# Expert weight units of four row blocks by 512 columns, and the fourth remainder of a group split between two engines

## The reference, cut to what matters

```python
order = jnp.argsort(flat_e)
tok = order // TOP_K
sizes = jnp.bincount(flat_e, length=N_EXPERTS).astype(jnp.int32)
xs = t[tok]
hid = jax.nn.silu(lax.ragged_dot(xs, w1, sizes)) * lax.ragged_dot(xs, w3, sizes)
y = lax.ragged_dot(hid, w2, sizes) * top_p.reshape(-1)[order][:, None].astype(h.dtype)
```

## Time and profile before

| what | value |
|---|---|
| median of 3 timed runs | 6221.68 us (6217.64 to 6225.43) |
| the profiled execution, its own time | 6225.65 us |
| its span, first to last instruction | 6223.8 us |
| granted TensorE clock, mean of the span | 0.923 of full speed |
| PE busy | 5444.2 us (87%) |
| DVE, ACT, POOL busy | 2205.8, 1831.2, 1837.4 us |

### The profile page before, as it was taken

How to read it: one execution, slowest core, us unless ns; L and a number is a source line. 1 busy time by engine, 2 the same in 40 slices (tenths; PEclk the granted TensorE clock), 3 DMA queues, 4 the chain that set the end, 5 groups by cost and what they waited for, 6 DMA issues and landing times. The chain is left out here.

```text
span 6223.8 us, 73697 instructions
## 1 busy us (share of the span) xinstructions
PE 5444.2 (87%) x29832; PEld 4546.9 (73%) x29833; DVE 2205.8 (35%) x1993; ACT 1831.2 (29%) x1481; POOL 1837.4 (30%) x506
## 2 busy tenths in 40 slices
PE   3778879997989978887999769999999999999996
PEld 3527657775778754565776568999989998899985
DVE  8344321112202123523112223333355335753356
ACT  0113111113312121211111223333445334653344
POOL 0130111112444322120111052532534253642534
PEclk5779889998999988898999789999999999999997
DMA  9201011122333330010112065555568556985568
GB/s 387 83 0 25 17 34 46 46 86 68 91 112 98 102 104 10 14 27 22 46 46 84 19 233 193 188 189 188 195 227 276 192 182 217 332 274 182 189 223 296
DMA packets 733656, 831.56 MB, mean 134 GB/s; under 512 B 17394, under 2 KB 648306, under 8 KB 733170
## 3 DMA queue, kind: packets, MB, share of 16 engines
q1 hardware_dynamic: 724386, 794.49, 39.4%
q0 software_dynamic: 4608, 16.78, 0.8%
q10 hardware_dynamic: 4560, 18.88, 0.8%
HBM read 784.99 MB, written 45.09 MB: 133 GB/s over the span
## 5 line engine op out<-in xcount | busy, mean ns | idle before, releaser
L1821 POOL TENSOR_TENSOR e_w_lo<-e_raw,e_w_hi 128x2048 fp32r<-128x2048 f32 x170 | 1074.1, 6330 | 1480.8 <-ACT e_w_hi L1759 1480.8
L247 POOL TENSOR_TENSOR w_lo<-w_raw,w_hi 128x1024 fp32r<-128x1024 f32 (+1 forms) x260 | 612.4, 2357 | 2487.4 <-ACT w_hi L242 2487.4
L253 PE MATMUL banks<-h_hi,w_hi 128*128 128x512 f32 x2688 | 1086.0, 404 | 191.7 <-POOL w_lo L247 127.0
L254 PE MATMUL banks<-h_lo,w_hi 128*128 128x512 f32 x2688 | 1056.7, 393 | 0.0
L255 PE MATMUL banks<-h_hi,w_lo 128*128 128x512 f32 x2688 | 1055.8, 393 | 0.0
L253 PE MATMUL banks<-e_x_hi,e_w_hi 128*128 128x256 f32 x3584 | 1020.7, 285 | 35.1 <-issue 23.9
L254 PE MATMUL banks<-e_x_lo,e_w_hi 128*128 128x256 f32 x3584 | 1019.6, 284 | 0.0
L255 PE MATMUL banks<-e_x_hi,e_w_lo 128*128 128x256 f32 x3584 | 1019.4, 284 | 0.0
L1759 ACT ACTIVATE e_w_hi<-e_raw 128x2048 fp32r<-128x2048 f32 x340 | 648.5, 1912 | 540.2 <-PE banks L255 530.2
L253 PEld LDWEIGHTS banks<-h_hi,w_hi 128*128 128x128 f32 x2688 | 511.0, 190 | 326.8 <-issue 154.6
L253 PEld LDWEIGHTS banks<-e_x_hi,e_w_hi 128*128 128x128 f32 x3584 | 692.0, 193 | 38.3 <-issue 26.0
(11 more groups left out here) (276 smaller groups left out, 6224.6 us busy)
## 6 DMA issues: line engine op xcount, KB each, us to landing
e_raw<-in_moe_w_dram SPq DMA_DIRECT2D x510, 1024.0 KB, 5.1
w_raw<-in_ffn_w_dram SPq DMA_DIRECT2D x120, 512.0 KB, 3.9
w_raw<-in_w_in_dram SPq DMA_DIRECT2D x108, 512.0 KB, 4.1
ada_w<-in_ada_w_dram SPq DMA_DIRECT2D x16, 3072.0 KB, 12.7
e_io<-row_scratch SPq DMA_DIRECT2D x13, 1024.0 KB, 6.8
y_scratch<-e_io ACTq DMA_DIRECT2D x12, 1024.0 KB, 4.2
x_res<-x_scratch SPq DMA_DIRECT2D x16, 512.0 KB, 5.8
w_br<-in_w_branch_dram SPq DMA_DIRECT2D x64, 128.0 KB, 3.9
```

What stands on the lines that cost most here:

```text
L247: pool.tensor_tensor(m.w_lo[b][:, 0:kt, :], m.w_raw[b][:, 0:kt, :], m.w_hi[b][:, 0:kt, :].bitcast(F32), ALU.subtract).then_inc(s.lo_ready, 1)
L253: pe.matmul(out, wh, rh, start=first, stop=False)
L254: pe.matmul(out, wh, rl, start=False, stop=False)
L1821: eng.tensor_tensor(flat(w_lo[u]), flat(raw[n % RING]), flat(w_hi[u]).bitcast(F32), ALU.subtract).then_inc(lo_sem[u % 2], 1)
```

## The change

Two things are changed together, in the up units of both kinds of item.

A unit now holds four of the eight row blocks (`KH`) by all 512 columns of the group, instead of eight by 256: units 0 and 1 are the two row halves of w1, units 2 and 3 those of w3. A narrow item's up unit is then 12 matmuls of 512 columns instead of 24 of 256; a wide item's is 48 of 256 as before. A sum is complete only after two units, so both halves' `silu` wait for unit 1 and both halves' `gated` wait for unit 3. PE may not begin a new group's w1 before both silus, nor its w3 before both products, of the group before.

The fourth remainder of a group (u = 3) is made in two halves of 1024 columns, one by POOL (`rest13`) and one by DVE (`rest_half`). The orders of ACT, DVE and PE around a group are written anew, and PE's loop over the groups of a narrow item is unrolled.

```diff
-        return flat(t).rearrange("p (k n) -> p k n", k=KT)
+        return flat(t).rearrange("p (k n) -> p k n", k=KH)
...
+    def half_out(q, h, width):
+        if width == HALF:
+            return m.ps[:, 2 * q + h, :]
+        return m.ps[:, 2 * q, width * h:width * (h + 1)]
...
-                w = (a.moe_w1, a.moe_w3)[u % 2]
+                w = (a.moe_w1, a.moe_w3)[u // 2]
...
-                             w[e2, ds(ex, 1)].rearrange("o (k p) n -> p (o k) n", p=P)[:, :, P * FGRP * i + 2 * P * (u // 2):
-                                                                                      P * FGRP * i + 2 * P * (u // 2) + 2 * P]
+                             w[e2, ds(ex, 1)].rearrange("o (k p) n -> p (o k) n", p=P)[:, KH * (u % 2):KH * (u % 2) + KH,
+                                                                                      GW * i:GW * (i + 1)]
...
             def silu(item, i, h, width):
-                act.wait_ge(s.mm_done, UNITS * item + 4 * i + 2 * h + 5)
+                act.wait_ge(s.mm_done, UNITS * item + 4 * i + 6)
...
             def gate_blocks(item, width):
-                for i in range(NFG - 1):
-                    for h in range(2):
-                        silu(item, i, h, width)
-                        unit13(item, i + 1, 2 * h)
-                        unit13(item, i + 1, 2 * h + 1)
...
+                for i in range(NFG):
+                    last = i == NFG - 1
+                    for u in range(4):
+                        if last:
+                            unit2(item, u)
+                        else:
+                            unit13(item, i + 1, u)
+                        if u == 0:
+                            for h in range(2):
+                                silu(item, i, h, width)
...
-            eng.tensor_tensor(flat(w_lo[u]), flat(raw[n % RING]), flat(w_hi[u]).bitcast(F32), ALU.subtract).then_inc(lo_sem[u % 2], 1)
+            cols = slice(0, D) if u == 3 else slice(0, 2 * D)
+            eng.tensor_tensor(flat(w_lo[u])[:, cols], flat(raw[n % RING])[:, cols], flat(w_hi[u])[:, cols].bitcast(F32),
+                              ALU.subtract).then_inc(rest_sem[u % 2], 1)
...
+            def unit_waits(item, i, u):
+                if u == 0:
+                    pe.wait_ge(s.x_lo, item + 1)
+                    pe.wait_ge(s.silu, 2 * (NFG * item + i) + 2)
+                if u == 2:
+                    pe.wait_ge(s.hid, 2 * (NFG * item + i) + 2)
+                pe.wait_ge(rest_sem[u % 2], 2 * (NFG * item + i) + u // 2 + 3)
+                if u == 3:
+                    pe.wait_ge(s.rest_half, 2 * (NFG * item + i) + 4)
...
-                for k in range(KT):
-                    last = mm3(pe, m.ps[:, 2 * q + h, 0:2 * P], xg_hi[:, k, 0:P], xg_lo[:, k, 0:P], hi[:, k, :], lo[:, k, :],
-                               k == 0, k == KT - 1)
+                for k in range(KH):
+                    last = mm3(pe, m.ps[:, 2 * q, :], xg_hi[:, KH * kh + k, 0:P], xg_lo[:, KH * kh + k, 0:P], hi[:, k, :], lo[:, k, :],
+                               u % 2 == 0 and k == 0, u % 2 == 1 and k == KH - 1)
...
-                turn_hidden(item, 0, 0)
-                with pe.Fori(1, NFG) as i:
...
+                for i in range(1, NFG):
                     up_unit(item, i, 0)
-                    up_unit(item, i, 1)
-                    turn_hidden(item, i - 1, 1)
-                    up_unit(item, i, 2)
-                    up_unit(item, i, 3)
-                    turn_hidden(item, i, 0)
...
+                    for h in range(2):
+                        turn_hidden(item, i - 1, h)
+                    for u in range(1, 4):
+                        up_unit(item, i, u)
...
-                dve.wait_ge(s.mm_done, UNITS * item + 4 * i + 2 * h + 6)
...
+                dve.wait_ge(s.mm_done, UNITS * item + 4 * i + 8)
...
+                        for u in (0, 2):
+                            rest13(dve, item, 1, u)
+                        for i in range(1, NFG):
+                            narrow_hidden(item, i - 1)
+                            rest_half(item, i)
+                            next_rests(item, i)
+                        narrow_hidden(item, NFG - 1)
```

More of the change, by code:

```diff
@@ L1855, in up @@
                     for u in range(4):
[L1856 to L1861, removed]
-                        hi, lo = by_k(w_hi[u]), by_k(w_lo[u])
-                        for f in range(2):
-                            for k in range(KT):
-                                last = mm3(pe, m.ps[:, 2 * q + h, ITEM * f:ITEM * (f + 1)], hi[:, k, P * f:P * f + P],
-                                           lo[:, k, P * f:P * f + P], xg_hi[:, k, :], xg_lo[:, k, :], k == 0, k == KT - 1)
+                        q, kh = u // 2, u % 2
@@ new lines, in up @@
+                        unit_waits(item, i, u)
+                        hi, lo = by_k(w_hi[u]), by_k(w_lo[u])
+                        for f in range(FGRP):
+                            for k in range(KH):
+                                last = mm3(pe, m.ps[:, 2 * q + f // 2, ITEM * (f % 2):ITEM * (f % 2 + 1)], hi[:, k, P * f:P * f + P],
+                                           lo[:, k, P * f:P * f + P], xg_hi[:, KH * kh + k, :], xg_lo[:, KH * kh + k, :],
+                                           u % 2 == 0 and k == 0 and f % 2 == 0, u % 2 == 1 and k == KH - 1 and f % 2 == 1)
@@ L1983, in rest2, with rest_half, narrow_hidden, next_rests @@
                 dve.tensor_tensor(flat(w_lo[c % 4]), flat(raw[n % RING]), flat(w_hi[c % 4]).bitcast(F32), ALU.subtract).then_inc(s.lo2, 1)
+            def rest_half(item, i):
+                n = 4 * i + 3
+                dve.wait_ge(s.hi_ready, UNITS * item + n + 1)
+                dve.tensor_tensor(flat(w_lo[3])[:, D:2 * D], flat(raw[n % RING])[:, D:2 * D], flat(w_hi[3])[:, D:2 * D].bitcast(F32),
+                                  ALU.subtract).then_inc(s.rest_half, 2)
+            def narrow_hidden(item, i):
+                for h in range(2):
+                    gated(item, i, h, 2 * P)
+                for h in range(2):
+                    turned(item, i, h)
+            def next_rests(item, i):
+                if i < NFG - 1:
+                    for u in (0, 2):
+                        rest13(dve, item, i + 1, u)
+                else:
+                    for c in range(3):
+                        rest2(item, c)
             x_rest(1)
@@ L1992, in _ @@
                     with dve.If(left < P + 1):
[L1993 to L2013, removed]
+                        for u in (0, 2):
+                            rest13(dve, item, 1, u)
[4 more added lines that the diff above has]
+                        narrow_hidden(item, NFG - 1)
                     with dve.Else():
[L2015 removed]
+                        for u in (0, 2):
+                            rest13(dve, item, 1, u)
+                        for i in range(1, NFG):
                             for h in range(2):
[L2017 to L2018 removed]
+                                hidden(item, i - 1, h)
+                            rest_half(item, i)
+                            next_rests(item, i)
                         for h in range(2):
                             hidden(item, NFG - 1, h)
[L2021 to L2022 removed]
+                    rest2(item, 3)
                     x_rest(item + 2)
@@ L2027, in _ @@
                         rest13(dve, item + 1, 0, 2 * h)
+                    rest_half(item + 1, 0)
 def combine_phase(nc, m, a, l):
```

41 lines of the change are left out of this document (21 added, 20 removed).

## The result

| what | before | after |
|---|---|---|
| median (4 runs each) | 6222.12 us | 6328.68 us (6324.26 to 6333.42) |
| ratio, 95% interval | | 1.0172 [1.0154, 1.0189] |
| profiled execution, its span | 6225.65, 6223.8 us | 6330.42, 6328.6 us |
| granted TensorE clock, mean | 0.923 | 0.918 |
| POOL busy | 1837.4 us | 1408.6 us |

The change makes the kernel 107 us slower. I had forecast 22 us, with 6275 as the upper end of the range.

The account below looks back on a forecast made before the run. PE was taken to bound wide items and POOL narrow ones; narrow items +4, wide items +14.3, end of phase -1.0 and clock +5 gave +22 us, 6248 by the profiled execution, forecast 6244 us, range 6210 to 6275.

Parts of the forecast that it names:

- the term for code loading: Item starts on PE: nothing in the sum; as a rival, long stops from the longer program, 0.13 to more than 15 us.
- two gaps of 8.47: Two item starts before the change where PE stood 8.47 us with no visible wait, against 2.3 elsewhere.
- 166 more rows on PE: PE's program is 166 rows longer, since the loop over groups is unrolled.
- nine more x 6.1: Code loading's case of the long stop at all eleven later item starts: +55 us, 6299.
- Wide tail: End of a wide item's up units: transposes start 1.79 us later, eight items, +14.3 us.
- Narrow period: One group of a narrow item's up units: 13.2 us after the change, against 13.3 before.
- The chain: Narrow group: silus, ACT's rounding, POOL's unit 1 remainder, DVE's unit 2 remainder, then the product; 13.2 us a period.
- Narrow item: Whole narrow item: -0.6 + 4.1 - 2.1 - 1.0 + 0.3 = +0.7, taken as +1 us; four items +4.
- Clock: Lower granted PE clock after longer idle gaps at wide items' ends: bounds 0 and 14 us, taken as +5.
- The rival "faster": Narrow groups: DVE's unit 2 remainder doesn't meet POOL at work; 6182, or 6208 with half the groups so; chance 0.12.
- the 11.4 that PE needs: PE's own work in a narrow group after the change: 11.4 us, down from 12.0.
- the 2391 ns of the earlier trace: Price taken for POOL's half remainder, from the nearest row of 1024 columns; used as 2.39 us.

Follow-up runs that it names:

- the rolled kernel: The kernel after with PE's narrow group loop as a loop again, the wait for `y_in` one unit earlier; 6246.90 us, 1.0042 of before.
- experiments 4 and 5: The kernel after with 75 and with 150 never-executed transposes behind the narrow item's down units; 6256.21 us, 1.0061, and 6344.27 us, 1.0205 of before.
- 2: The kernel before with only PE's narrow group loop unrolled; 6245.66 us, 1.0041 of before.
- 3: The rolled kernel with 259 never-executed transposes behind the narrow item's down units; 6266.90 us, 1.0075 of before.
- Experiment 9: The rolled kernel with products ahead of splits at wide items' ends, and narrow items' products before DVE's next unit 2 remainder; 6203.77 us, 0.9973 of before.
- Experiment 10: Experiment 9 without the split of the fourth remainder, POOL making all of it; 6230.07 us, 1.0015 of before.

## Why the prediction was wrong

**The step that failed is the term for code loading.** The sum put it at nothing, and the rival that had it got a chance of 0.13 and "nine more x 6.1". I had the signs in hand, two gaps of 8.47 with nothing to wait for and 166 more rows on PE, and weighed them by the length of the code. Measured: the rolled kernel, with the same waits, has gaps 77.0 us shorter and runs 81.8 us faster. Against before, the gaps cost 64.4: six starts became long, not nine, and the two long ones grew by 5.7 each. A stop is not one price either: from wide to wide 14.1 - 2.3 = 11.8, from wide to narrow 8.0 - 2.0 = 6.0. In the stop of 14.13 three packets were fetched, in those of 8.04 after and of 8.47 before two; so 6.1 was too small where a stop fetches more pieces.

The Trainium skill, "Runtime: NRT & Kernel Launch", section "Instruction fetch mechanics", has blocks of 16 KiB, 256 instructions, and room for 2048 on PE, which is eight; the packets of 16.4 KB agree, and at the starts between the first wide items experiments 4 and 5 came out as a count with eight said. No run here shows the number eight itself. Its advice in the same section, that kernels prefer full unrolling where possible, does not carry over to one loop inside a loop with branches, where a jump back is left: unrolling it cost 82 us here. The rule by which a piece is kept or dropped stays open: the count doesn't give the 6 to 10 us behind narrow items in 2 and 3.

**The rest of the sum is tested by the rolled kernel**, which has no long starts: 6246.9, against 6244 forecast. Part by part it is less good than that looks.

- *Wide tail*, +1.79 x 8: right. Measured 2.57 - 0.78 = 1.79, at all eight.
- *Narrow period*, 13.2: 13.36. The chain runs as I wrote it, PE waits 1.7 us at the transposes, and POOL is idle 4.5 us a period.
- *Narrow item*, +1: mis-sized. In after the only one that starts without a long stop takes 142.6 us, against 138.0 before; in the rolled kernel they take 143. The first product stands 20.06 us behind the item's start, where I had 18.7; the second comes 14.9 to 15.4 later, where I had 13.2, with 3.4 to 6.8 us of it at the lower clock; the other periods cost 0.16 each (0.23 in the rolled kernel); the last one, 11.4 to the second product, is as forecast within 0.3. Four items make about +20 instead of +4.
- *Clock*, +5: not separable. The rolled kernel has 61.4 us at the lower level, before had 37.5, and 34 of the 61.4 lie ahead of the second product of the narrow items, counted above.
- What I left out was a gain: rolled, the two long starts of before go too, -12.5 us. 14.3 + 20 - 12.5 = 22, beside 26.4 measured: errors that cancelled.

For after itself, whose profiled execution took 104.8 us more than before's: the starts are 64.4 and the tails 14.3. The four narrow items, less their long starts, are 3.1, 3.3, 4.6 and 3.0 us longer, together 14. The wide items took up to 4 us more than their starts and tails explain, together about 7; it is mostly in the three behind the first, 4 us in one of them (260.5, against 242.8 before, less 11.8 and 1.8), and fits the 2.6 us lost at the lower clock behind a long stop. Some 5 us are left without a place.

**The rival "faster"** named the right point: POOL and DVE meeting. Experiment 9 takes the chain away and gains, but a period is 12.2 us there and not the 11.4 that PE needs. PE waits 0.5 us or less a period for POOL, whose two remainders take 10.55 and stand 1.6 for ACT's rounding. Experiment 10 shows that POOL's work counts there; what else sets the 12.2 isn't tested.

## What to carry to other kernels

Idle time at "issue" behind a jump, together with instruction packets, points to code loading. What it costs depends on where the branches lie and not only on how long the code is: before unrolling a loop inside a loop with branches, count the pieces that one pass touches, and price the worst case at every pass. When work is moved off an engine, first follow the chain of the period; halving POOL's remainder was worth 0 us with the chain in place and 26 without it. Where two engines take turns, look at which one starts first: 1.2 us more work on one of them went with items 13 us longer.

## What the runs showed of the hardware

- The same 2048-column remainder on DVE took 2.29 us alone and 4.42, 4.73 and 6.70 beside POOL's, each time to 2.15 us behind POOL's end. The half remainder on POOL took 2.65 us as the last of the phase, where 0.44 us of DVE's remainder were left at its start, and 4.21 in the narrow item, where it stands behind all that is left of DVE's: the 2391 ns of the earlier trace rows was a price for an engine that nobody held up.
- 151 instructions that are never executed made a kernel 72 us faster (experiment 4), and 301 made it 16 us slower (experiment 5), where the gaps at the starts account for 1.
- With fewer and larger rows (DMA packets 558604, against 733656) the narrow stretch moved 331 GB/s at a share of 0.94, against 328 at 0.99; kernel 9 moves 355 at 0.97.
